# Token-wise output and down projections and norms in a two-layer hybrid block, with the first up group cut to four chunks

## What is computed

```python
for l in range(DEPTH):                       # DEPTH = 2
    mod = (silu(c) @ ada_w[l] + ada_b[l]).reshape(bsz, N_MOD, D_MODEL)[:, :, None, :]
    shift_m, scale_m, gate_m = mod[:, 0], mod[:, 1], mod[:, 2]
    shift_f, scale_f, gate_f = mod[:, 3], mod[:, 4], mod[:, 5]
    h = rms_norm(x, mix_pre_g[l]) * (1.0 + scale_m) + shift_m
    y = hybrid_mixer(h, ..., w_in[l], ..., w_out[l])   # window attention beside a linear recurrence
    x = x + gate_m * rms_norm(y, mix_post_g[l])
    h = rms_norm(x, ffn_pre_g[l]) * (1.0 + scale_f) + shift_f
    y = conv_ffn(h, ffn_w_up[l], ..., ffn_w_down[l])   # up to 6144, conv, gelu * value, down from 3072
    x = x + gate_f * rms_norm(y, ffn_post_g[l])
```

## Time and profile before

| | us |
|---|---|
| three runs | 1177.88, 1184.41, 1183.84 |
| median | 1183.84 |
| span of the profiled execution | 1171.8 |
| median less span | 12.0 |
| PE busy in the span | 1145.2 |

### The profile page before, as it was taken

The page is one execution under the profiler, slowest core; times in us unless marked ns, Lnnn a source line. Parts: engine busy times, 40 slices in busy tenths (PEclk is TensorE's granted clock), DMA queues, the critical chain, the costliest instruction groups (busy, mean ns, idle before and its releaser), DMA issues.

```text
span 1171.8 us, 16207 instructions
## 1 busy us (share of the span) xinstructions
PE 1145.2 (98%) x6616; PEld 999.9 (85%) x6616; DVE 823.0 (70%) x1265; ACT 557.0 (48%) x918; POOL 51.9 (4%) x110
## 2 busy tenths in 40 slices
PE   6999899999999999999999999999999999999996
PEld 6986799988888888888999779998888888888896
DVE  7989978688778787676487884577833665355644
ACT  4488936454134432444248994545522443233441
POOL 3000110000110011000000000000000000000000
PEclk7999999999999999999999999999999999999998
DMA  9833453334866568454112230304323323233212
GB/s 358 334 118 108 160 201 109 114 103 149 292 229 189 165 202 307 138 154 134 55 37 108 73 103 6 109 5 160 106 90 99 99 90 108 91 94 104 90 55 72
DMA packets 44970, 155.79 MB, mean 133 GB/s; under 512 B 5088, under 2 KB 7392, under 8 KB 44896
## 3 DMA queue, kind: packets, MB, share of 16 engines
q1 hardware_dynamic: 34384, 116.48, 29.9%
q0 software_dynamic: 10368, 37.75, 9.8%
q10 hardware_dynamic: 144, 0.52, 0.2%
HBM read 152.64 MB, written 2.10 MB: 132 GB/s over the span
## 4 chain that ended last, share of the span: by engine, by line
PE 90%; DVE 6%; ACT 2%; issue 1%; DMA 1%; SPq 0%; DVEq 0%; ACTq 0%
PE ps L1910 63%; PE ps L1935 24%; PE ps L2035 2%; DVE sb_stage L1179 1%; DVE sb_wL L1173 1%; ACT sb_sq L710 1%; DVE sb_xc L1424 1%; DMA sb_raw<-in_w 0%; PE ps L2173 0%; ACT sb_scr L710 0%; DVE sb_scr L1310 0%; DVE sb_tiny L1406 0%; DVE sb_mL L1472 0%; ACT sb_wH L605 0%; DMA sb_sq<-in_pos 0%
## 5 line engine op out<-in xcount | busy, mean ns | idle before, releaser
L1910 PE MATMUL ps<-sb_hH,sb_wH 128*128 128x512 f32 x800 | 313.0, 391 | 0.6 <-ACT sb_xc L729 0.6
L1910 PE MATMUL ps<-sb_hL,sb_wH 128*128 128x512 f32 x800 | 311.4, 389 | 0.0
L1910 PE MATMUL ps<-sb_hH,sb_wL 128*128 128x512 f32 x800 | 311.4, 389 | 0.0
L605 ACT ACTIVATE sb_wH<-sb_raw 128x1024 fp32r<-128x1024 f32 x174 | 181.7, 1053 | 127.0 <-DMA sb_raw<-in_w 126.8
L1173 DVE TENSOR_TENSOR sb_wL<-sb_raw,sb_wH 128x1024 fp32r<-128x1024 f32 x174 | 211.7, 1219 | 23.4 <-ACT sb_wH L605 23.2
L1910 PEld LDWEIGHTS ps<-sb_hH,sb_wH 128*128 128x128 f32 x800 | 150.2, 188 | 36.3 <-issue 5.2
L1910 PEld LDWEIGHTS ps<-sb_hH,sb_wL 128*128 128x128 f32 x800 | 150.2, 188 | 31.2
L1910 PEld LDWEIGHTS ps<-sb_hL,sb_wH 128*128 128x128 f32 x800 | 150.2, 188 | 30.7
L1774 DVE SCALAR_TENSOR_TENSOR sb_R<-ps,sb_par,sb_R 128x511 f32<-128x511 f32 x84 | 62.9, 748 | 91.8 <-ACT sb_R L1060 91.8
L1060 ACT ACTIVATE sb_R<-ps,sb_par 128x512 f32<-128x512 f32 x84 | 65.2, 776 | 107.1 <-PE ps L1910 106.9
L1910 PE MATMUL ps<-sb_mL,sb_wH 128*128 128x512 f32 x288 | 112.1, 389 | 0.0
(11 more groups left out here) (261 smaller groups left out, 1731.8 us busy)
## 6 DMA issues: line engine op xcount, KB each, us to landing
sb_raw<-in_w SPq DMA_DIRECT2D x174, 512.0 KB, 3.6
sb_adaw<-in_ada POOLq DMA_DIRECT2D x42, 512.0 KB, 4.8
sb_stage<-in_ada SPq DMA_DIRECT2D x24, 512.0 KB, 14.3
sb_vw<-in_ada POOLq DMA_DIRECT2D x20, 512.0 KB, 4.9
sb_side<-in_w SPq DMA_DIRECT2D x8, 512.0 KB, 5.1
sb_raw<-in_w SPq DMA_DIRECT2D x8, 384.0 KB, 14.3
sb_stage<-in_ada POOLq DMA_DIRECT2D x6, 512.0 KB, 4.8
sb_x<-in_x SPq DMA_DIRECT2D x4, 512.0 KB, 5.6
```

The costliest lines, as they stand in the source:

```text
L605: nc.scalar.activation(high_of(n), raw_of(n), ACT.Copy).then_inc(w_hi, 1)
L1910: return nc.tensor.matmul(out, a, b, start=start, stop=stop, **kw)
```

## The change

The out and down projections are turned round. The stationary operand is now a 128x128 block of activations (128 tokens, `mH` or `mL`), the moving one a row of 512 output features of the weights, so the output has 128 tokens in the partitions and 512 features along the free axis (`token_products`). A stage has four token tiles t and two feature halves fh; the host lays these weights out anew (`by_tokens`). All of their matmuls are 512-wide, 24 to a chunk, as before in whole chunks. In the program, 256-wide matmuls fall from 2,496 to 960 and 512-wide ones rise from 3,270 to 4,038.

y, x and the norms are by token too. A sum of squares over features is now along the free axis: an ACT square with an accumulated sum. The factor of a token is one number for each partition, so nothing is spread by PE. The gate, which was one number for each partition, becomes a row: ACT's queue writes it to DRAM, element by element, and reads it back into all partitions. x is loaded a second time, by tokens (`xt`). The normalised x is turned back to features for the next projection by PE transposes, eight for each token tile (`transposes`), after which ACT scales and shifts the lower four blocks and DVE the upper four.

The up projection's first group has 4 halved chunks where it had 6. The side slots are gone: all chunks run through the ring, and a chunk of a token stage is released only when the last token tile has used it. The code that turns from one stage to the next is one chain for each token tile (`tile_chains`, in ACT's and DVE's list, shown in part by the rows below).

```diff
 GRP = 6
+UG = 4
 SLOTS_W = 6
...
+FH = 2
+KP = KT // 2
...
+            sp.wait_ge(tmp_ready, KT)
+            for t in range(QT):
+                sp.dma_start(x_tile(t), A["xt"][tile_of(t), :]).then_inc(xt_in, 16)
+            for n in range(2 * GRP, DEPTH * NCH):
+                refill(n)
+            for t in range(QT):
+                for fh in range(FH):
+                    sp.wait_ge(x_upd, tile_no(DEPTH - 1, 1, 0) + 2 * t + fh)
+                    sp.dma_start(A["out"][tile_of(t), fh * SEQ:(fh + 1) * SEQ], x_tile(t, fh)).then_inc(stored, 16)
...
+            def gate_write(row):
+
+                act.wait_ge(fac_ready, row + 1)
+                with nc.allow_non_contiguous_dma(reason="a column of factors becomes a row"):
+                    act.dma_start(A["grow"][row].rearrange("(k p) -> p k", p=P),
+                                  fac[:, row // 2, 1 + 2 * (row % 2), :]).then_inc(g_out, 16)
+
+            def gate_read(row):
+
+                act.wait_ge(g_out, 16 * [1, 2, 4, 4][row])
+                act.dma_start(gate_row.rearrange("p a b -> p (a b)"),
+                              A["grow"][row:row + 1, :].broadcast_to([P, D])).then_inc(g_in, 16)
...
+                nc.scalar.activation(sqo[t % 2], src, ACT.Square,
+                                     accum_out=ysum[fh][:, t:t + 1]).then_inc(y_sq, 1)
...
+            def x_root(l, k, t):
+
+                act.wait_ge(x_upd, tile_no(l, k, t))
+                S.mark(nc.scalar.activation(y_tile(t), x_tile(t), ACT.Square, accum_out=xsum[:, t:t + 1]))
+                self_wait()
...
+            def x_scaled(l, k, t):
+
+                act.wait_ge(x_rs, tile_no(l, k, t))
+                nc.scalar.activation(y_tile(t), x_tile(t), ACT.Copy, scale=xrs[:, t:t + 1]).then_inc(x_hat, 1)
...
+                    last = nc.scalar.activation(y_tile(t)[:, kt * P:(kt + 1) * P], bank(6)[:, kt * P:(kt + 1) * P],
+                                                ACT.Identity, bias=shifts[:, kt:kt + 1], scale=gains[:, kt:kt + 1])
...
+            def y_gate(l, k, fh, t):
...
+                    TT(gated_y(k, t, fh), tm_bank(OUT_, fh, t), gate_row[:, fh, :], ALU.mult).then_inc(y_read, 1)
...
+                for fh in range(FH) if k == 1 and l == DEPTH - 1 else [None]:
+                    STT(out=x_tile(t, fh), in0=gated_y(k, t, fh), scalar=rs, in1=x_tile(t, fh),
+                        op0=ALU.mult, op1=ALU.add).then_inc(x_upd, 1)
...
+                    last = TS(y_tile(t)[:, kt * P:(kt + 1) * P], bank(7)[:, (kt - 4) * P:(kt - 3) * P],
+                              gains[:, kt:kt + 1], shifts[:, kt:kt + 1], ALU.mult, ALU.add)
...
-                factors(l, 1)
-                late(8, 2)
-                late(10, 1)
-                add_square(l, 0, 0, 0)
+                y_gate(l, 0, 0, 0)
+                late(8, 1)
+                y_gate(l, 0, 0, 1)
+                late(9, 2)
+                y_gate(l, 0, 0, 2)
                 late(11, 2)
-                add_square(l, 0, 1, 0)
-                all_added(l, 0, 0)
...
+                    ahead = [[5], [6, 7], [8, 9], [10, 11]]
+                    for r in range(4):
+                        fh, pair = divmod(r, 2)
+                        units(down_no(g, 2 * r))
+                        units(down_no(g, 2 * r + 1))
+                        for c in ahead[r]:
+                            lo_chunk(B + down_no(g, 0) + c)
+                        for t in (2 * pair, 2 * pair + 1):
+                            y_evict(l, DOWN0 + g, fh, t)
...
+                stage = IN_ if k else UP_
+                pairs = GRP // 2 if k else UG // 2
...
+                            if i == 0 and kt % 4 == 0:
+                                pe.wait_ge(t_hi, part_no(l, k, 2 * h + 1, kt // 4))
+                                pe.wait_ge(t_lo, part_no(l, k, 2 * h + 1, kt // 4))
...
+                            if h == 0 and (i, kt) == (0, KT - 1):
+                                transposes(l, k, 2)
+                            if h == 0 and (i, kt) == (1, KT - 1 if k else KT // 2 - 1):
+                                transposes(l, k, 3)
+
+            def transposes(l, k, t):
+
+                pe.wait_ge(x_hat, tile_no(l, k, t))
+                if t:
+                    pe.wait_ge(tmp_a, tile_no(l, k, t - 1))
+                    pe.wait_ge(tmp_d, tile_no(l, k, t - 1))
+                for kt in range(KT):
+                    last = nc.tensor.transpose(bank(6 + kt // 4)[:, kt % 4 * P:(kt % 4 + 1) * P],
+                                               y_tile(t)[:, kt * P:(kt + 1) * P], ident[:, :])
+                    if kt % 4 == 3:
+                        last.then_inc(tr_done, 1)
...
+                pair_mm(acc, a, w, opens, False)
+                pair_mm(acc, a, wl, False, False)
...
+                last = pair_mm(acc, al, w, False, kt == KT - 1)
+                if t == QT - 1 and kt % 2:
+                    last.then_inc(chunk_done, 1)
+                elif kt == KT - 1:
+                    last.then_inc(tm_done, 1)
+
...
+            def finishing(l, stage, k):
+
+                fh = 1
+                turning = k == 0 or l + 1 < DEPTH
+                first = KT // 2 if stage == OUT_ else 0
+                for t in (0, 1):
+                    for kt in range(first, KT):
+                        if t == 0 and kt % 2 == 0 and kt >= first:
+                            pe.wait_ge(w_lo, w_no(l * NCH + tm_first(stage) + KP * fh + kt // 2))
+                        token_products(l, stage, fh, t, kt, kt == 0)
+                for t in (2, 3):
+                    if stage == OUT_:
+                        pe.wait_ge(y_read, read_no(l, stage, 0, t - 2))
+                    elif t == 3:
+                        pe.wait_ge(y_read, read_no(l, stage, 0, 0))
+                    for kt in range(KT // 2):
+                        token_products(l, stage, fh, t, kt, kt == 0)
+                for t in (2, 3):
+                    if turning:
+                        transposes(l, k, t - 2)
+                    for kt in range(KT // 2, KT):
+                        token_products(l, stage, fh, t, kt, False)
...
-            def half_sums(h, at_, src, opens, closes, parts=2):
-
-                for t in range(2):
-                    for g in range(parts):
-                        first = g * HALF + t * P
-                        last = part_mm(bank(STAT_BANK[h])[:, at_ + t:at_ + t + 1], src[:, first:first + P], ones[:, 0:1],
-                                       opens and t == 0 and g == 0, closes and g == parts - 1)
-                return last
-
-            def half_spread(b, h, rs):
-
-                for t in range(2):
-                    last = mm(bank(b)[:, t * P:(t + 1) * P], rs[:, 2 * h + t:2 * h + t + 1].broadcast_to([P, P]),
-                              ident[:, :], True, True)
...
+    def by_tokens(w):
+        return w.reshape(KP, 2, P, FH, SEQ).transpose(3, 0, 2, 1, 4).reshape(KT, P, KT, P)
```

1036 lines of the change are left out of this document (372 added, 664 removed).

## The result

The changed kernel takes 1172.26 us (median of 20 runs, 1166.90 to 1175.62) against 1176.01 us of the kernel before (20 runs, 1173.28 to 1185.73). The ratio is 0.9943 with an interval of 0.9922 to 0.9963, a gain of 0.6%, some 6.7 us; the two medians alone lie 3.8 us apart, the two means 7.0. The prediction was 1159 us, from 1150 to 1172, and a gain of 24.8 us by its sum. The sign is right, the size is not, and the time lies just above the range.

What follows compares the result with a forecast made beforehand. PE's own list was taken to set the time. Terms -10.1, -30.4, +10.4, +9.0, -5.6, +1.5 and +0.4 sum to -24.8 us: span 1171.8 becomes 1147.0, with 12.0 around it 1159 us, range 1150 to 1172.

Steps and rivals of the forecast that it cites:

- Width, -10.1: Out, up and down matmuls on PE: 1,536 256-wide become 768 512-wide, each pair saving 0.0131 us, 10.1 us in all.
- Rival (a): A 512-wide matmul with activations stationary takes as long as two 256-wide ones, giving 1169 us; chance 0.10.
- Statistics, -30.4: At the norms between stages, PE's sums, spreads and waits for low parts all go, saving 30.4 us.
- tail, -5.6: After the last eviction, 11.9 us to the end shrinks to 6.3, saving 5.6 us.
- Transposes, +10.4: Three norms by four tiles add twelve groups of eight PE transposes, 0.87 us each, 10.4 us in all.
- Rival (c): Transposes do not overlap behind a wait and cost 275 ns each, giving 1175 us; chance 0.03.
- New waits, +9: PE waits on ACT and DVE at out-to-up and down-to-in boundaries: 8.3 us plus hand-overs, taken as 9.
- Unit loads, +1.5: Late unit loads in layer 0's first two down groups hold low parts that PE awaits: 1.5 us, bounds 0 and 4.4.
- Rival (d): Unit loads slow to 14.3 us under bursts of weights, 18 us lost at each of two places: 1193 us; chance 0.04.
- Rival (b): Each tile's chain on ACT, 7.0 us against PE's 5.4, is the bound; waits doubled, 1168 us; chance 0.12.
- Cost nothing, or little: Gate-row write +0.4 us for its issue; its reading, the second load of x and the ring taken as hidden.
- 12.0 around the span: Time taken to lie outside the profiled span, added to the predicted span of 1147.0 us to give 1159 us.

Runs made afterwards that it cites:

- e8_order_gates: Changed kernel with attention pieces of the out projection split between column sums and layer 1's two gate-row writes moved out of its in projection: 1157.85 us, ratio 0.9817.
- e6_before_writes: Kernel before plus two unread writes of 1,024 single elements on ACT's queue in layer 1's in projection: 1177.44 us, ratio 1.0032.
- e9_finer: Changed kernel with split attention pieces, one more piece of 12 split in both layers, and layer 1's gate-row writes moved: 1158.12 us, ratio 0.9838.
- e3_units: Changed kernel with the last three units of layer 0's out projection moved on DVE behind tile 1's update of x: 1169.54 us, ratio 0.9930.
- e4_xt: Changed kernel with the second load of x moved later on SP's queue, behind chunk 17: 1179.28 us, ratio 1.0004 to the kernel before.
- e5_all: Changed kernel with attention pieces split, layer 1's gate-row writes moved, three units moved and the second load of x later: 1170.07 us, ratio 0.9939.
- e7_before_order: Kernel before with its 256-wide attention pieces put together in the changed kernel's order, so column sums stand in a row: 1178.28 us, ratio 1.0002.
- e1_order: Changed kernel with attention pieces of 12 matmuls split into 6 and 6 between the column sums, as in before: 1162.24 us, ratio 0.9884.
- e2_gates: Changed kernel with layer 1's two gate-row writes moved to layer 0's second and layer 1's first down group: 1160.52 us, ratio 0.9861.
- e10_short_units: Changed kernel with pieces split, gate writes moved, and layer 0's eight late out-projection units cut to 8 of 1,024 columns: 1151.79 us, ratio 0.9788.

## Why the prediction missed, step by step

**Width, -10.1: right.** 192 512-wide matmuls of a down group take 43.52 us, 0.2267 each, with activations as the stationary operand. Rival (a) is dead. By the figures of the Trainium skill ("TensorE: Matmul & The Clock Gate", Back-to-back issue gap), which that section gives for an isolated matmul, a pair would save 6 cycles, 2.5 ns by estimate (2.6 in the prediction); the rows give 13.1.

**Statistics, -30.4, and tail, -5.6: right.** What the three norms are over is mostly the waits and the clock of the next paragraphs. The stretch from layer 1's first whole up chunk to the end is 376.9 against 376.3. The chain behind the last matmul is the one predicted, from the last eviction to the last update of x (DVE's timeline, as in the earlier trace rows):

```profile
1167.54 0.68 DVE L1169 TENSOR_TENSOR sb_y<-ps,sb_y 128x512 f32<-128x512 f32 x1
...
1169.73 1.42 DVE L1202 SCALAR_TENSOR_TENSOR sb_x<-sb_scr,sb_tiny,sb_x 128x512 f32<-128x512 f32 x2
```

From the eviction's start to the end of the span it is 6.1 us, by the steps 6.3.

**Transposes, +10.4: nearly.** Groups of eight take 0.92 and 1.06 on the chain above; at 1.06 for every one the term would be 12.7. Rival (c), 2.2 a group, did not come.

**New waits, +9: mis-sized.** Layer 1's out to up is 1.9 over, layer 0's 4.0. PE's waits at the three norms are 6.0, 3.4 and 1.7 us, 11.1 together, where I had 4.2, 3.4 and 0.7, so well below the 18 that I named as a sign of being wrong. The view of PE's waits has 5.3 for the first transposes of layer 0, where I had 2.4. The step of this term that failed is "eight times 1.15": I gave DVE its units without their loads, though the term on unit loads counted just these for the down groups. The 2.8 us of waiting for loads are about that difference. The other two waits came to 0.7 where I had 1.8, so the waits are 1.8 over; what is left of the 4.0 is, by estimate, 0.5 of transposes and 1.7 of PE near half its clock behind the wait (0.56 from 194 to 198). In layer 1 the waits are 1.0 of the 1.9. At down to in the longest wait, for a high part, is 2.3 (L666), and the line of the table with it is right within 0.4 us.

**Unit loads, +1.5: not in the changed kernel,** where the down groups run at 0.2267 without a break. The mechanism came up in the profile of `e8_order_gates`, with one load too late by 4.68 us and 1.8 us of PE's wait for a low part. Rival (d) named such loads too, but for the down groups; in the changed kernel they came late ahead of tile 0. Rival (b), doubled chains for every tile, would have put the third line of the table over, and it is not.

**"Cost nothing, or little": the step that failed.** I put the gate row's write beside the 2.1 us of a 0.5 KB load, with 14.3 as the worst case, and both times asked only who waits for its reading. It lands after 10 to 12 us, but what it costs is not its own waiting: the loads of weights that run beside it take 8 to 11 us in place of 3.5. No row of before has a scattered write, and the small load of the earlier trace rows is a poor likeness: it has 128 elements, the gate row 1,024. With the order of the pieces, which has no term at all, this is the 6.9 and 10.8 us by which layer 1's attention is over in the two profiles of the changed kernel, and `e8_order_gates` is not.

**The clock.** The prediction took the earlier trace rows at 1.00 as a property of the kernel. It is one of the execution, too: in layer 0's attention the changed kernel lost 8.7 us in one profile and 0.9 in another. That is most of the 12.0 us between its two profiled spans, and `e6_before_writes` shows such a loss without the change. The times of before vary in the same way, 1172.3 to 1188.6 in all its runs. The range of 22 us was made of priced terms alone, with 3 us for the spread of the runs; this spread by itself is some 9 us for the changed kernel and 12 for the one before.

**The base.** With the 1.8 us that every run shows, the sum would have given 1148.8, and the miss would have been 23.5 us. The error of 10.2 us in "12.0 around the span" hid the rest of it; the three runs, two of them near 1184, were not runs of the profiled execution.

**Open.** Why PE's clock falls in layer 0's attention in some executions and not in others is not settled. It fell for most of that stretch in one profile of the changed kernel and in those of `e9_finer` and `e6_before_writes`, for parts of it in the other profile of the changed kernel and in those of `e3_units`, `e4_xt`, `e5_all` and `e7_before_order`, and not in those of before, `e1_order`, `e2_gates`, `e8_order_gates` and `e10_short_units`. `e6_before_writes` has no gate row's write in layer 0, so the write is not the reason. The edits make it rarer at most: one run in four of `e1_order`, of `e9_finer` and of `e10_short_units` was 7 to 11 us above the others.

## What to carry to other kernels

A DMA that costs its own queue nothing can cost its neighbours: ask of a new transfer how many elements it has, not only how many bytes, and place it where the loads beside it have slack. When an edit merges pieces of wide matmuls, look at what they separated: here the wide matmuls behind 40 thin ones in a row, and those behind PE's waits of 4.6 and 5.3 us, ran in part at the lower clock, so such a place was paid for twice. And before a span is turned into a time, compare it with the spans of several runs.
